# A decoder layer on one core: TensorE two expert pairs behind VectorE instead of one, with eight diagonals instead of four

## The chip, the cores and the metric

The kernel runs on one core of one Trainium2 chip. The metric is the device time of one execution in microseconds (us); less is better.

## What is computed

One decoder layer on 1024 tokens of width 1024, in float32:

```python
proj = x @ w_in                                  # split in q,k,v of attention and q,k,v,b,a,z of DeltaNet
o_attn = sliding_window_sink_attention(q_a, k_a, v_a, attn_sinks)      # window 128, 8 heads
o_dn   = gated_delta_rule(q_d, k_d, v_d, g, beta)                      # 4 heads of 128, chunks of 64
x1 = layer_norm(ALPHA * x + concat(o_attn, o_dn) @ w_out)
# PEER, per block of 128 tokens
q = (x1 @ w_query); s = q . sub_keys             # 16 lists of 128 scores for each token
vals, idx = top_k(s, 16); best, pos = top_k(vals[a] + vals[b], 16)     # 8 heads x 16 = 128 experts a token
u, v = expert_u[expert], expert_v[expert]        # rows of 1024 each
h = gelu(sum_d x1[d] * u[d]) * softmax(best)
x2 = layer_norm(ALPHA * x1 + sum_k h[k] * v[k])
```

Every token thus gathers 128 rows u and 128 rows v, 8 KB for each pair of rows.

## The kernel before

The tokens are worked in 8 blocks of 128 (NB). Each block has two kinds of work, and the kernel interleaves them on every engine:

- **The mixer**: input projection, attention, DeltaNet, output projection, first LayerNorm, expert queries, key scores and top-k. Its weights come in chunks of 1 MB: four stay in SBUF (KEPT), and the others are streamed by SyncE through two buffers `chunk`, each loaded when the product that used the buffer before is done (`chunk_used`).
- **The experts**: 128 gathers of 1 MB a block (128 rows of 8 KB each). GpSimd issues them (L445) into a **ring of 8 places** (RING, `ring`). Gather j uses place j % 8, and GpSimd waits until the gather that had the place before was added (`added`, L440; `ring_free`). The numbers of the experts come from the top-k, in four parts of 32 gathers (`staged`).

The experts go in **pairs** of gathers, 64 a block. For a pair VectorE makes two dot products of u with the tokens (L1421), ScalarE the GELU and the weighting (L994, L997) and two diagonal matrices of 128 x 64 (L1001, `diag`, DIAGS places), and TensorE multiplies the rows v by the diagonals into the PSUM sums `expert_sum` (L757, 8 matmul records). Its last matmuls raise `added`, and only they free the two places of the ring.

The order is written out by hand. `mix()` exists once for each engine and walks through the mixer with calls of `mark(name)`. The tables EARLIER and OWN say how many pairs belong to each mark: a block's first 15 pairs are done in OWN, from `top1` to `pick3`, while its own top-k still runs, and the other 49 in EARLIER, from `rope` to `pick0`, beside the mixer of the next block. At each mark VectorE and ScalarE do the pairs up to number b. **TensorE stands one pair behind**: its marks call `experts(n, b - 1)`, so that at a mark it works the pairs up to b - 1 and stops short of the one that VectorE does there.

So the ring's four pair places are, by the program, in these states when an engine stands at a mark: done by VectorE and not yet added; loaded; on the way.

Four places in the order are spoken of below.

- **The block's boundary**: the marks `sel3`, `rest3`, `pick3` (no mixer product of TensorE between them), then the `Fori` branch, then TensorE waits for `roped` (VectorE's L1187, L1188), transposes (L548, L551), and comes to the marks `rope`, `gates`, `taps1`, then the scores (L560). There are seven boundaries; five are branches back of the loop, and the first and the last lie between code that stands one behind the other.
- **The first LayerNorm**: marks `out3`, `scale1`, `shift1` without a product between, then the wait for `x1_ready` (VectorE's L1127), the transposes L504, mark `x1_T`, and the query chunks (L493).
- **The turn-over** after mark `pick0`: TensorE adds the last pairs of the older block (`experts(n - 1, PAIRS)`), VectorE reads the sums (L1439) and stages the tokens, and the pairs start from 0 again.
- **The tail**: the last block's experts from pair 15 on, with no mixer beside them.

```python
RING = 8
DIAGS = 4
OWN = {name: 1 for name in ("top1",) + NEXT_IN + AFTER_IN}
    act.wait_ge(*weighted.at(n, j + 1))
    act.wait_ge(*added.at(n, j - DIAGS + 1))
    pool.wait_ge(*added.at(n, ring_free(j)))
```

Of the kernel before, what the change touches and what calls it, by code (L numbers as in the profile page):

```python
# [28 lines left out]
P = 128  # L29
SEQ, D = 1024, 1024  # L30
NB = SEQ // P
# [4 lines left out]
DH, DK = 4, 128  # L36
CHUNK = 64
TAPS = 4
PH, KEYS, TOPK = 8, 128, 16
# [14 lines left out]
PART = SLOTS // 4  # L54
DIAGS = 4
KEPT = (0, 1, IN_CHUNKS, IN_CHUNKS + 1)
# [7 lines left out]
for _name, _width in (("ident", P), ("one", 1), ("upto", P), ("strict", P), ("same16", P), ("off32", P),  # L64
                      ("off64", P), ("same64", P), ("band", 2 * P), ("iota", TOPK),
                      ("freq", HALF), ("eps_ln", 1), ("eps_rms", 1), ("eps_l2", 1), ("ln_qscale", 1),
                      ("halves", P // 2)):
    CONSTS[_name] = (_at, _at + _width)
    _at += _width
# [3 lines left out]
def constants():  # L73

    i, j = np.arange(P)[:, None], np.arange(P)[None, :]
    same = lambda w: (i // w) == (j // w)
# [7 lines left out]
        "same16": same(16), "off32": same(32) & ~same(16), "off64": same(64) & ~same(32),  # L84
        "same64": same(CHUNK),
        "band": np.where((c > i) & (c <= i + P), 0.0, NEG),
# [56 lines left out]
def build(nc, io):  # L143
    ctx = ExitStack()
    with ctx:
# [9 lines left out]
        bank = [ctx.enter_context(nc.psum_tensor(f"bank{i}", [P, 512], F32)) for i in range(6)]  # L155
# [53 lines left out]
        def col(i, k=1):  # L209
            return small[:, i:i + k]  # L210
# [250 lines left out]
        def _(pe):  # L461
# [81 lines left out]
            def mix(n, mark, turn_over, early=False, onward=True):  # L543
# [53 lines left out]
                pe.matmul(bank[1][:, 0:DH], C["upto"], col(S_G, DH), start=True, stop=True)  # L597
                pe.matmul(bank[1][:, DH:2 * DH], C["same64"], col(S_G, DH), start=True, stop=True).then_inc(g_sums.sem, 1)
                pe.matmul(bank[0][:, :], ones, tile(A_UG), start=True, stop=True).then_inc(g_sums.sem, 1)
# [178 lines left out]
            for c in range(IN_CHUNKS):  # L778
                in_chunk(0, c, early=True)
            mix(0, Marks(own=lambda a, b: experts(0, b - 1)), lambda n: None, early=True)  # L780
            after_own = taken[0]
            with pe.Fori(1, NB - 1) as n:
                mix(n, Marks(lambda a, b: experts(n - 1, b - 1), lambda a, b: experts(n, b - 1)), turn_over)
                assert taken[0] == after_own
            mix(NB - 1, Marks(lambda a, b: experts(NB - 2, b - 1), lambda a, b: experts(NB - 1, b - 1)), turn_over, onward=False)
            pe.wait_ge(*out_ready.at(NB - 1, 0))
# [739 lines left out]
```

## Time and profile before

| | before |
|---|---|
| median of 3 runs | 3373.32 us |
| range of the 3 runs | 3371.08 to 3377.5 us |
| the profiled execution, its own time | 3375.34 us |
| its span in the trace | 3373.5 us |
| TensorE busy | 2459.0 us (73%) |
| VectorE busy | 2230.8 us (66%) |
| ScalarE busy | 1155.5 us (34%) |
| GpSimd busy | 1177.7 us (35%) |
| moved by DMA | 1254.83 MB, mean 372 GB/s |
| mean granted clock of TensorE | 0.857 |

The span is what the trace covers. The execution's own time is 1.8 us longer. A busy share is a mean over stages with different limits, so it doesn't name the bound.

### The profile page before, as it was taken

To read this page: it belongs to the slowest core of one execution; us is meant where nothing else is said; L and a number is where in the kernel's file an instruction comes from. 1 tells how busy PE (TensorE), PEld (TensorE's weight loads), DVE (VectorE), ACT (ScalarE), POOL (GpSimd) and SP (SyncE) were. 2 spreads that over 40 slices of the span, in tenths; PEclk is the share of its full clock that TensorE was granted. 3 is DMA by queue.
4 is the path that set the end of the run, shared out by engine and by line. 5 is a ranking of instruction groups with operands and counts; after the bars stand their busy time and mean duration, and the time that the engine had idled before them with its cause. 6 is when DMAs were issued, how large, how long until landed. Compare 5 with 4: busy or idle time off the path is not lost.

```text
span 3373.5 us, 40986 instructions
## 1 busy us (share of the span) xinstructions
PE 2459.0 (73%) x11840; PEld 1374.0 (41%) x11840; DVE 2230.8 (66%) x5593; ACT 1155.5 (34%) x3499; POOL 1177.7 (35%) x1028
## 2 busy tenths in 40 slices
PE   8786778857788577885788677786778867775554
PEld 6663335523355233552345333453335523351111
DVE  3267755877558765687657775587755876569444
ACT  3213532325323443225332252333532344322222
POOL 0022443224422344233542244322442234423543
PEclk8698988978889798898989888897898979887777
DMA  7049999989999899998999989998999999989997
GB/s 321 7 176 416 394 405 395 382 336 416 404 392 393 350 398 408 401 392 348 416 397 379 398 343 418 381 385 345 415 404 400 385 389 411 411 360 350 410 420 327
DMA packets 174948, 1254.83 MB, mean 372 GB/s; under 512 B 20184, under 2 KB 20312, under 8 KB 23520
## 3 DMA queue, kind: packets, MB, share of 16 engines
q0 software_dynamic: 147456, 1073.81, 78.4%
q1 hardware_dynamic: 25056, 172.66, 12.4%
q10 hardware_dynamic: 2176, 5.36, 0.4%
q8 instruction: 106, 1.74, 0.2%
q14 instruction: 154, 1.26, 0.1%
HBM read 1247.56 MB, written 4.19 MB: 371 GB/s over the span
## 4 chain that ended last, share of the span: by engine, by line
PE 31%; DMA 31%; DVE 17%; issue 10%; ACT 8%; POOL 1%; DVEq 0%; POOLq 0%; ACTq 0%; SPq 0%
DMA ring<-in_uv,expert_used 20%; PE expert_sum L757 12%; DMA chunk<-in_weights 10%; PE bank L493 7%; DVE ring L1421 7%; PE bank L485 5%; ACT diag L1001 2%; PE bank L499 2%; POOL ring L445 1%; ACT h_raw L997 1%; PE bank L504 1%; ACT L994 1%; PE bank L586 1%; PE bank L674 1%; PE bank L673 1%
## 5 line engine op out<-in xcount | busy, mean ns | idle before, releaser
L445 POOL DMA_INDIRECT ring<-in_uv,expert_used x1024 | 1177.5, 1150 | 2165.7 <-PE expert_sum L757 1661.3
L757 PE MATMUL expert_sum<-ring,diag 128*64 128x512 f32 x4096 | 1202.6, 718 | 651.3 <-ACT diag L1001 651.1
L1421 DVE CUSTOM_DVE_ANT_0 ring<-ring,x_pair 128x1024 f32<-128x1024 f32 x1024 | 1231.3, 1222 | 586.9 <-DMA ring<-in_uv,expert_used 579.7
L757 PEld LDWEIGHTS expert_sum<-ring,diag 128*64 128x64 f32 x4096 | 296.6, 156 | 1305.7 <-issue 742.0
L994 ACT ACTIVATE h_raw<-h_raw 128x2 f32<-128x2 f32 x512 | 104.4, 204 | 1542.8 <-DVE h_raw L1421 1542.3
L1001 ACT ACTIVATE diag<-const,h_raw 128x64 f32<-128x64 f32 x1024 | 298.5, 338 | 1.2 <-ACT h_raw L997 1.2
L493 PE MATMUL bank<-oT,chunk 128*128 128x128 f32 x1824 | 226.1, 285 | 37.8 <-DMA chunk<-in_weights 37.0
L997 ACT ACTIVATE h_raw<-h_raw,gate_used 128x1 f32<-128x1 f32 x1024 | 245.6, 286 | 16.7
L493 PEld LDWEIGHTS bank<-oT,chunk 128*128 128x128 f32 x1824 | 216.2, 198 | 70.6 <-DMA chunk<-in_weights 49.8
L493 PE MATMUL bank<-o_cat,chunk 128*128 128x128 f32 x1376 | 169.6, 283 | 36.4 <-DMA chunk<-in_weights 36.2
L493 PEld LDWEIGHTS bank<-o_cat,chunk 128*128 128x128 f32 x1376 | 161.7, 196 | 72.7 <-DMA chunk<-in_weights 62.8
L1144 DVE MAX8 arena<-arena 128x8 f32<-128x128 f32 (+1 forms) x384 | 103.7, 325 | 46.4 <-ACT arena L953 41.2
L499 PEld LDWEIGHTS bank<-arena 128*128 128x128 f32 x768 | 102.5, 213 | 59.0 <-issue 51.4
L499 PE MATMUL bank<-arena 128*128 128x128 f32 x768 | 114.6, 305 | 5.5 <-DVE arena L1286 1.6
L949 ACT COPY arena<-bank 128x512 f32<-128x512 f32 x32 | 18.7, 585 | 269.8 <-PE bank L493 269.8
L485 PE MATMUL bank<-chunk,o_cat 128*128 128x256 f32 x352 | 87.4, 405 | 16.2 <-DMA chunk<-in_weights 16.2
L994 ACT ACT_TABLE_LOAD x72 | 92.4, 1283 | 2.8 <-DVE h_raw L1421 1.6
L548 PE MATMUL bank<-const,arena 128*64 128x128 f32 x64 | 14.2, 399 | 107.9 <-DVE arena L1188 107.9
L485 PEld LDWEIGHTS bank<-chunk,o_cat 128*128 128x128 f32 x352 | 69.2, 202 | 38.6 <-DMA chunk<-in_weights 25.0
L1421 DVE DVE_READ_ACCUMULATOR2_ANT h_raw<- 128x1 f32 x1024 | 83.1, 81 | 0.0
L485 PE MATMUL bank<-kept,o_cat 128*128 128x256 f32 x256 | 74.5, 455 | 7.4 <-DMA kept<-in_weights 7.4
L1168 DVE SCALAR_TENSOR_TENSOR conv<-conv_in,conv_w,conv 128x128 f32<-128x128 f32 x288 | 77.8, 343 | 0.0
(237 smaller groups left out, 2539.7 us busy)
## 6 DMA issues: line engine op xcount, KB each, us to landing
chunk<-in_weights SPq DMA_DIRECT2D x137, 1024.0 KB, 10.0
ring<-in_uv,expert_used POOLq DMA_INDIRECT x1024, 11.7
ring<-in_weights SPq DMA_DIRECT2D x15, 1024.0 KB, 21.0
o_cat<-in_xT SPq DMA_DIRECT2D x8, 512.0 KB, 10.7
kept<-in_weights SPq DMA_DIRECT2D x4, 1024.0 KB, 19.1
x<-in_x SPq DMA_DIRECT2D x8, 512.0 KB, 13.6
out<-oT ACTq DMA_DIRECT2D x8, 512.0 KB, 10.2
sub_keys<-in_sub_keys ACTq DMA_DIRECT2D x1, 1024.0 KB
```

The source lines that it names most:

```text
L445: pool.indirect_dma_start(out=ring[:, (j % RING) * 2 * D:(j % RING + 1) * 2 * D], out_offset=None, in_=io["uv"], in_offset=bass.IndirectOf ...
L485: mm = pe.matmul(out, act[:, k, :], w[:, k, :], start=(k == 0), stop=(k == KT - 1))
L493: mm = pe.matmul(out, w[:, k, i * P:(i + 1) * P], act[:, k, :], start=(k == 0), stop=(k == KT - 1))
L499: mm = pe.matmul(out[:, hs], lhsT[:, hs], rhs[:, hs], start=True, stop=True)
L504: mm = pe.transpose(out[:, h * P:(h + 1) * P], in_[:, h * P:(h + 1) * P], ident)
L757: mm = pe.matmul(expert_sum[i][c * SPAN:(c + 1) * SPAN, :], diag[:, (j % DIAGS) * SPAN:(j % DIAGS + 1) * SPAN], ring3[:, j % RING, D + i * ...
L994: act.activation(h_raw[:, pair[0]:pair[1] + 1], h_raw[:, pair[0]:pair[1] + 1], ACT.Gelu).then_inc(gelued.sem, 1)
L997: act.activation(h_raw[:, j:j + 1], h_raw[:, j:j + 1], ACT.Copy, scale=gate_used[:, j:j + 1]).then_inc(weighted.sem, 1)
L1001: act.activation(diag[:, (j % DIAGS) * SPAN:(j % DIAGS + 1) * SPAN], C["halves"], ACT.Copy, scale=h_raw[:, j:j + 1]).then_inc(diag_ready.s ...
L1144: ins = dve.max(values[:, one[part]], one[2])
L1168: stt(out=convo[:, t, :], in0=conv3[:, t, k:k + P], scalar=conv_w[:, t * TAPS + k:t * TAPS + k + 1], in1=convo[:, t, :], op0=ALU.mult, op1 ...
L1421: dve.tensor_tensor_reduce(u, u, x_pair[:, (j % 2) * D:(j % 2 + 1) * D], 1.0, 0.0, ALU.mult, ALU.add, h_raw[:, j:j + 1]).then_inc(dotted.s ...
```

## The change

TensorE's marks take two pairs off instead of one, not below zero. At a mark it works the pairs up to b - 2, so that two pairs that VectorE has done stay unadded there. ScalarE's diagonals get eight places, 2 KB a partition instead of 1 KB; with them its wait at L1000 is for pair q - 4 instead of q - 2. `turn_over` and the last `experts` still work all pairs that are left.

To make room the constant `same64` goes. The sum of the gates over a chunk of 64, which was a product with it, becomes two products into the same place in PSUM, with `upto` (i <= j) and with `strict` (i > j), which together are `same64`.

```diff
-DIAGS = 4
+DIAGS = 8
...
-                      ("off64", P), ("same64", P), ("band", 2 * P), ("iota", TOPK),
+                      ("off64", P), ("band", 2 * P), ("iota", TOPK),
...
-        "same64": same(CHUNK),
...
-                pe.matmul(bank[1][:, DH:2 * DH], C["same64"], col(S_G, DH), start=True, stop=True).then_inc(g_sums.sem, 1)
+                pe.matmul(bank[1][:, DH:2 * DH], C["upto"], col(S_G, DH), start=True, stop=False)
+                pe.matmul(bank[1][:, DH:2 * DH], C["strict"], col(S_G, DH), start=False, stop=True).then_inc(g_sums.sem, 1)
...
-            mix(0, Marks(own=lambda a, b: experts(0, b - 1)), lambda n: None, early=True)
+            mix(0, Marks(own=lambda a, b: experts(0, max(b - 2, 0))), lambda n: None, early=True)
...
-                mix(n, Marks(lambda a, b: experts(n - 1, b - 1), lambda a, b: experts(n, b - 1)), turn_over)
+                mix(n, Marks(lambda a, b: experts(n - 1, max(b - 2, 0)), lambda a, b: experts(n, max(b - 2, 0))), turn_over)
...
-            mix(NB - 1, Marks(lambda a, b: experts(NB - 2, b - 1), lambda a, b: experts(NB - 1, b - 1)), turn_over, onward=False)
+            mix(NB - 1, Marks(lambda a, b: experts(NB - 2, max(b - 2, 0)), lambda a, b: experts(NB - 1, max(b - 2, 0))), turn_over, onward=False)
```

TensorE's program just behind the block's boundary, in the loop's body. L757 is a pair; L751 REGISTER_ALU stands ahead of pair 16, whose wait for its gather has a new value. Before:

```order
L757 MATMUL expert_sum<-ring,diag 64x512 x4
L752 REGISTER_ALU
L757 MATMUL expert_sum<-ring,diag 64x512 x4
L751 REGISTER_ALU
L752 REGISTER_ALU
L757 MATMUL expert_sum<-ring,diag 64x512 x4
L556 ISA
L557 REGISTER_ALU
L560 MATMUL bank<-k_keys,arena 128x256 x8
```

The same place in the change (its lines from 460 to 597 stand one lower):

```order
L757 MATMUL expert_sum<-ring,diag 64x512 x4
L752 REGISTER_ALU
L757 MATMUL expert_sum<-ring,diag 64x512 x4
L752 REGISTER_ALU
L757 MATMUL expert_sum<-ring,diag 64x512 x4
L555 ISA
L556 REGISTER_ALU
L559 MATMUL bank<-k_keys,arena 128x256 x8
L751 REGISTER_ALU
L752 REGISTER_ALU
L757 MATMUL expert_sum<-ring,diag 64x512 x4
```

Three pairs stand ahead of the scores in both. Before they are 14, 15 and 16; in the change they are 13, 14 and 15, and 16 has moved behind the scores.

TensorE's program at the turn-over: L718 are the last key scores, L514 rows for the second LayerNorm, L485 the next block's first two weight chunks. Before:

```order
L757 MATMUL expert_sum<-ring,diag 64x512 x4
L718 MATMUL bank<-sub_keys,arena 128x128 x4
L752 REGISTER_ALU
L757 MATMUL expert_sum<-ring,diag 64x512 x4
L767 REGISTER_ALU
L514 MATMUL bank<-k_keys,const 128x512 x4
L520 ISA
L485 MATMUL bank<-kept,o_cat 128x256 x8
L751 ISA
L752 ISA
L757 MATMUL expert_sum<-ring,diag 64x512 x4
L485 MATMUL bank<-kept,o_cat 128x256 x8
```

In the change:

```order
L757 MATMUL expert_sum<-ring,diag 64x512 x4
L718 MATMUL bank<-sub_keys,arena 128x128 x4
L752 REGISTER_ALU
L757 MATMUL expert_sum<-ring,diag 64x512 x4
L752 REGISTER_ALU
L757 MATMUL expert_sum<-ring,diag 64x512 x4
L767 REGISTER_ALU
L513 MATMUL bank<-k_keys,const 128x512 x4
L519 ISA
L484 MATMUL bank<-kept,o_cat 128x256 x16
L751 ISA
L752 ISA
```

Two pairs are left for the turn-over instead of one, and the next block's first pair stands behind two weight chunks instead of one.

## Rows read from the trace of the kernel before

**Rows 1.** The page: busy times of the engines.
```profile
PE 2459.0 (73%) x11840; PEld 1374.0 (41%) x11840; DVE 2230.8 (66%) x5593; ACT 1155.5 (34%) x3499; POOL 1177.7 (35%) x1028
```

**Rows 2.** The page's costliest groups: count | busy, mean ns | idle before, what ended it.
```profile
L757 PE MATMUL expert_sum<-ring,diag 128*64 128x512 f32 x4096 | 1202.6, 718 | 651.3 <-ACT diag L1001 651.1
L1421 DVE CUSTOM_DVE_ANT_0 ring<-ring,x_pair 128x1024 f32<-128x1024 f32 x1024 | 1231.3, 1222 | 586.9 <-DMA ring<-in_uv,expert_used 579.7
```

**Rows 3.** Stretches: us, busy of each engine, TensorE's granted clock, DMA share, GB/s.
```profile
1560.00:1700.00 140.00, 105.07 (x498) 49.63 (x499) 93.20 (x177) 65.66 (x198) 66.92 (x55) 0.92 1.01 418
3130.00:3330.00 200.00, 114.31 (x320) 29.27 (x320) 98.44 (x160) 46.42 (x200) 96.23 (x81) 0.76 1.01 420
1360.00:1410.00 50.00, 44.55 (x318) 33.33 (x318) 31.71 (x98) 13.38 (x44) 13.02 (x15) 1.00 0.98 396
```

**Rows 4.** The last chain in order of time, 1640 to 1680 us: start, us, what.
```profile
1647.72 1.22 DVE ring L1421
...
1650.26 3.56 PE expert_sum L757 x8
...
1655.82 11.82 DMA ring<-in_uv,expert_used
```

**Rows 5.** The same columns as rows 3, at four of the seven boundaries.
```profile
330.00:350.00 20.00, 13.87 (x58) 6.68 (x58) 19.69 (x48) 8.55 (x24) 8.96 (x8) 0.84 0.82 315
730.00:750.00 20.00, 12.61 (x51) 6.51 (x51) 15.51 (x41) 8.23 (x24) 5.29 (x4) 0.69 0.25 81
...
1530.00:1550.00 20.00, 8.29 (x34) 3.32 (x34) 11.76 (x36) 7.97 (x19) 2.58 (x3) 0.63 0.37 136
...
2740.00:2760.00 20.00, 14.72 (x58) 6.98 (x58) 19.59 (x46) 6.73 (x24) 9.74 (x8) 0.84 0.75 292
```

**Rows 6.** TensorE in order of time about 1541 us: start, us, instruction [idle before].
```profile
1519.88 3.68 PE L757 MATMUL expert_sum<-ring,diag 128*64 128x512 f32 x8 [5.54 <-ACT diag L1001]
1541.30 1.88 PE L548 MATMUL bank<-const,arena 128*64 128x128 f32 x8 [17.74 <-DVE arena L1188]
...
1543.54 4.19 PE L757 MATMUL expert_sum<-ring,diag 128*64 128x512 f32 x16
```

**Rows 7.** GpSimd, the gathers of the same stretch.
```profile
1524.37 1.97 POOL L445 DMA_INDIRECT ring<-in_uv,expert_used  x1 [5.00 <-PE expert_sum L757]
...
1546.82 0.94 POOL L445 DMA_INDIRECT ring<-in_uv,expert_used  x1 [19.24 <-PE expert_sum L757]
1548.06 0.94 POOL L445 DMA_INDIRECT ring<-in_uv,expert_used  x1 [0.30 <-PE expert_sum L757]
```

**Rows 8.** Line 445 alone, gathers issued from 1546 to 1549 us: time to landing.
```profile
DMA to landing us min/median/max: 5.7/6.5/7.4
```

**Rows 9.** VectorE in order of time, the second dot product of pair 17.
```profile
1551.09 1.21 DVE L1421 CUSTOM_DVE_ANT_0 ring<-ring,x_pair 128x1024 f32<-128x1024 f32 x1
```

**Rows 10.** All engines in order of time, at the first LayerNorm.
```profile
1353.20 1.28 DVE L1127 TENSOR_TENSOR x<-x,bank 128x512 f32<-128x512 f32 x2
...
1354.60 3.68 PE L757 MATMUL expert_sum<-ring,diag 128*64 128x512 f32 x8 [6.05 <-ACT diag L1001]
...
1358.21 1.97 PE L504 MATMUL bank<-const,x 128*128 128x128 f32 x8
```

**Rows 11.** Stretches as in rows 3, at three of the seven turn-overs.
```profile
1810.00:1840.00 30.00, 25.07 (x105) 14.06 (x103) 20.78 (x65) 10.86 (x24) 6.75 (x7) 0.89 0.84 339
2220.00:2250.00 30.00, 26.68 (x100) 15.00 (x97) 24.05 (x77) 10.27 (x23) 10.69 (x11) 0.83 0.99 407
...
3010.00:3040.00 30.00, 17.33 (x71) 7.69 (x71) 20.84 (x65) 10.16 (x23) 7.62 (x8) 0.71 0.72 282
```

**Rows 12.** All engines in order of time, a turn-over.
```profile
1417.59 2.78 DVE L1439 SCALAR_TENSOR_TENSOR oT<-x_pair,expert_sum 64x512 f32<-64x512 f32 x4 [6.96 <-PE expert_sum L757]
...
1431.11 3.68 PE L757 MATMUL expert_sum<-ring,diag 128*64 128x512 f32 x8 [4.63 <-ACT diag L1001]
...
1434.72 4.05 PE L485 MATMUL bank<-kept,o_cat 128*128 128x256 f32 x16
```

## The prediction

> **What bounds the kernel now.** I began with the page's busy times [rows 1]. No engine is above 73%, so none of them is the bound by itself. The two waits between TensorE and the experts are large [rows 2]: TensorE stood idle 651.3 us before pairs, for diagonals of ScalarE, and VectorE 579.7 us for gathers. The first invites the change: TensorE is held at a pair that isn't ready, while mixer work stands behind it in its program. Whether these waits cost time is for the DMA share to say.
>
> So I asked for stretches [rows 3]. With gathers alone, beside the mixer or without it, the DMA share is 1.01 and 418 to 420 GB/s are moved: that is what full looks like here. In the query chunks it is still 0.98. I read the chain of waits in such a stretch [rows 4] as a ring: dot product, diagonals, TensorE's pair, gather, 11.82 us until it lands, dot product again. One turn takes 20 us and serves four pairs, so 5 us a pair. A pair is 2.10 MB (two gathers of 1.05 MB), and at 419 GB/s that is 5.0 us. The 11.82 us are thus queueing behind the other gathers, and the bound is **bytes**. The 651.3 us of TensorE's waits mostly lie in stretches where DMA has no time to give.
>
> Time is then lost only where DMA runs dry. Taking 1.01 as full, the boundaries show it [rows 5]: the share is 0.25 and 0.37 over 20 us at two that are branches of the loop, and 0.82 and 0.75 at the first and the last, where no branch stands. Holes: (1.01 - 0.37) x 20 = 13 us, (1.01 - 0.25) x 20 = 15 us, 4 us and 5 us. The other three branches look like these two. A smaller hole is at the turn-over [rows 11], 5 us at the largest of the first six and 0.6 us at the smallest.
>
> Why the boundary is dry: TensorE adds pair 13 at 1519.88 us and then has nothing to do until `roped`; it adds pair 14, whose dots were long done, at 1543.54 [rows 6]. GpSimd issues no gather between the second of pair 17 (2.3 us after the row at 1524.37) and the first of pair 18 at 1546.82 [rows 7]. In these 20 us the four places hold pair 14 (done, not added), 15, 16 and 17, and when 17 has landed DMA has nothing left.
>
> **The change, part by part.**
>
> *One more place held at the boundary.* At `pick3` TensorE now stops after pair 12. Pairs 13 and 14 are both unadded while it waits for `roped`, and the gather of pair 17, which before went out at 1524.37, needs the place of 13. It goes out where before 18 did, at 1546.82. DMA's last work before the hole is one pair shorter and the hole ends at the same point of the program, so it grows by one pair: 5.0 us. I check it by landings. Gathers issued into the empty queue took 5.7 and 7.4 us [rows 8]; the second, issued at 1548.06, lands at 1555.5. Pair 17's second dot product started at 1551.09 [rows 9], so VectorE comes 4.4 us later. Both ways agree to 0.6 us, and the hole exists at all seven boundaries: 7 x 5.0 = **+35 us**, bounds 7 x 4.4 = 31 and 7 x 7.4 = 52, if a whole landing were to show. The rows are nearest to 5.0, since DMA is full again right behind the hole (rows 3's first stretch follows it).
>
> The Trainium skill, "DMA: Bandwidth & Descriptors", section Anatomy of one DMA, fits a transfer as 2.0 us and its bytes at 436 GB/s. By that the two gathers would land 2.0 + 2 x 2.4 us behind the first issue, at 1553.6, VectorE would lose 2.6 us, and the seven would cost 18 us in place of 35, an estimate. The landings of 5.7 and 7.4 us are longer than the page has it, so I keep the rows. The same page's Specifications give 358 GB/s as the HBM limit of a core; by that a pair would be 5.9 us and the seven 41 us, but the rows move 418.
>
> *A place held longer everywhere else.* In the full stretches it costs nothing, and what hides it is the queue. Pair j is added one mark later, yet TensorE no longer waits there for ScalarE. The mixer product ahead of the mark needs VectorE's step ahead of pair j + 1's dots, so it comes right behind j's own diagonals. If the shift were a whole pair (5 us), the gather would still be issued with more than one pair on the way: 11.82 us of queue less 5. The cover ends where TensorE holds pairs over 10 us, as at the boundary. The query chunks come near: TensorE is busy 44.55 of 50 us there [rows 3]. Bounds: 0, and one pair per block, 7 x 5.0 = 35 us. I take 0, since the share is 0.98 there.
>
> *TensorE's head start.* At the first LayerNorm x1 is ready after L1127 (1353.20 + 1.28 = 1354.5 us), but pair 54 is first, 3.68 us, and the transposes start at 1358.21 [rows 10]. With the change the pairs ahead of the transposes are older and done, so the transposes start near 1354.6: 3.6 us sooner, and the query chunks behind them too. At the turn-over VectorE waited 6.96 us for the last sum, which hangs on these chunks [rows 12]. It can have up to 3.6 us of that back, and the dry time there shrinks, no further than its size. The first six holes, from (1.01 - share) x 30, were 0.6 to 5.1 us, on average 2.7 us when capped at 3.6; the seventh, with a share of 0.72 [rows 11], exceeds the cap. That is 6 x 2.7 + 3.6 = 20 us at most, and 0 at least. The head start must outlive seven weight chunks, each of which waits for DMA, so I take two thirds: **-14 us**. Later at the turn-over pair 0 stands behind two weight chunks; the 4.63 us for which TensorE waited there [rows 12] now hold the second (4.05 us, the last row there), so pair 0 isn't added later.
>
> *ScalarE and the diagonals.* The wait at L1000 gets four more places and two instructions of the sequencer go. It was no wait before: TensorE's pair begins where the diagonals end. The whole stretch from the dot product's start to TensorE's is 2.54 us [rows 4], of which at most 0.1 us goes, and only in a dry stretch does it count. Bounds 0 and -0.1 x 14 = -1.4 us; I take 0. What is late next is the gather itself.
>
> *The constant.* One more product of 128 x 4 in a block of 400 us, under 0.3 us each: at most 2 us, hidden by DMA, 0. The constants' load is 64 KB shorter at the start, 0.2 us by 419 GB/s, beside the weights: 0.
>
> *The tail* has no marks; TensorE there only waits for diagonals, as before: 0.
>
> Sum, against the profiled execution of 3375.3 us: + 35 - 14 = +21, 3396 us. The median of the three runs is 2 us lower, so I predict **3394 us** for the median. About 0.2% (7 us) is what a measurement of this kernel can tell from no change.
>
> **The rivals.**
>
> *A. The shorter ring also runs dry in the chunk stretches.* From the queries to `rest3` TensorE holds pairs behind products and chunk loads. If one pair's worth of queue goes in each of seven blocks, and the head start is used up by it, the sum is 35 + 35 = +70, 3443 us; half of it with the head start kept is about +38. For it: the share is 0.98, so the queue is already near its end, and two pairs held leave two. Against: with fewer gathers queued the weight chunks land sooner, and TensorE is back sooner.
>
> *B. No change.* The hole grows by less than I say, because the first gather into an empty queue lands fast. With 2.6 us instead of 5.0 at each boundary: 18 - 14 = +4, 3377 us. Against: rows 8 and 9.
>
> *C. Faster.* The mechanism is TensorE's hold at unready pairs, in the stretch from the first LayerNorm to the third chunk of the next block. If the head start is 3.6 us at the LayerNorm and 4.6 us more at the wait for pair 0 [rows 12], and all of it comes out at the end of a block, it is 7 x 8.2 = 57 us against 35: -22, 3351 us. It decides from 5.0 us of recovered time a block. For it: VectorE and TensorE both wait at the turn-over. Against: time can only come back where DMA was dry, and the dry time outside the boundaries is some 3 us a block.
>
> *D. The change doesn't do what it says*: the place of a diagonal or the branch decides the order and TensorE's pairs come where they were. The program's order speaks against it; I give it nothing.
>
> **How the numbers follow.** My forecast (3380 to 3410) has 0.50, A 0.23, B 0.12, C 0.15. The range reaches over B and into C's smaller half, and up to the middle of A: 3362 to 3430. Leaving out half of A and the better half of C leaves out some 0.18. Faster by over 0.2% is C, 0.15; within 0.2% is B, 0.12; slower is the forecast and A, 0.73.
>
> **What would show it.** Right: the 20 us stretch at each boundary is drier by 5 us (a share of 0.12 instead of 0.37); GpSimd issues pair 17 only behind `roped`, and VectorE waits some 4 us for it at `taps1`; L504 starts right behind L1127; TensorE's wait for ScalarE at L757 falls well below 651.3 us without a gain; full stretches still show 1.01. Wrong: the share at the boundaries is unchanged (B); the query chunks show shares of 0.9 and less, or VectorE's waits for gathers grow there by 5 us a block (A); the distance between two boundaries, 400 us now, shrinks (C).

## The result, and the profile after

| | before | after |
|---|---|---|
| median | 3372.94 us (3371.08 to 3377.5, 4 runs) | 3408.47 us (3404.27 to 3414.98, 4 runs) |
| ratio, 95% interval | | 1.0105 (1.0085 to 1.0125) |
| profiled execution, own time and span | 3375.34, 3373.5 us | 3406.38, 3404.5 us |
| TensorE's mean granted clock | 0.857 | 0.844 |
| moved by DMA | 1254.83 MB, 372 GB/s | 1254.81 MB, 369 GB/s |

The change costs 35 us. It moves the same bytes and its busy times are nearly the same. The page after, busy times and costliest groups, against [rows 1, 2]:

```profile
PE 2462.1 (72%) x11856; PEld 1395.9 (41%) x11856; DVE 2239.3 (66%) x5593; ACT 1143.3 (34%) x3499; POOL 1150.0 (34%) x1028
...
L1421 DVE CUSTOM_DVE_ANT_0 ring<-ring,x_pair 128x1024 f32<-128x1024 f32 x1024 | 1237.8, 1224 | 823.7 <-DMA ring<-in_uv,expert_used 817.1
L757 PE MATMUL expert_sum<-ring,diag 128*64 128x512 f32 x4096 | 1175.4, 708 | 416.4 <-ACT diag L1001 416.2
```

TensorE's wait for diagonals fell from 651.1 to 416.2 us, and VectorE's wait for gathers rose from 579.7 to 817.1. One fell by 235 us, the other rose by 237, and the kernel is slower. This is the first reading: **a wait that shrinks is no gain if it only moves to the engine that feeds the ring.**

The stretches after, columns as in [rows 3, 5]. The first three answer to rows 3, the other four to the boundaries of rows 5, each taken at the same distance from its `roped` (the boundaries come at other times now):

```profile
1580.00:1720.00 140.00, 110.61 (x496) 54.00 (x496) 88.93 (x160) 65.20 (x192) 57.79 (x52) 0.85 0.99 404
3160.00:3360.00 200.00, 111.92 (x322) 28.46 (x320) 98.26 (x161) 46.42 (x200) 98.22 (x80) 0.77 1.01 420
1363.00:1413.00 50.00, 43.16 (x299) 33.04 (x298) 25.86 (x83) 11.36 (x40) 12.38 (x12) 0.97 0.95 375
...
319.60:339.60 20.00, 15.08 (x58) 7.05 (x58) 14.53 (x39) 7.81 (x22) 8.33 (x7) 0.77 0.52 200
722.10:742.10 20.00, 12.66 (x50) 6.50 (x50) 12.11 (x36) 7.89 (x19) 4.86 (x5) 0.68 0.22 71
1535.20:1555.20 20.00, 8.73 (x35) 3.71 (x36) 12.42 (x39) 8.34 (x21) 2.16 (x3) 0.61 0.22 77
2755.90:2775.90 20.00, 15.81 (x63) 7.47 (x65) 13.83 (x36) 6.19 (x20) 8.01 (x8) 0.84 0.55 205
```

Full is full still (0.99 and 1.01). The boundary is drier: 0.82 to 0.52 and 0.75 to 0.55 where no branch stands (6 and 4 us), 0.25 to 0.22 and 0.37 to 0.22 at branches. The query chunks fell from 0.98 to 0.95.

TensorE in order of time about the boundary at 1546.3 us, against [rows 6]:

```profile
1523.52 2.77 PE L757 MATMUL expert_sum<-ring,diag 128*64 128x512 f32 x6
1546.47 1.89 PE L547 MATMUL bank<-const,arena 128*64 128x128 f32 x8 [20.18 <-DVE arena L1188]
1548.15 0.64 PE L550 MATMUL bank<-const,arena 128*64 128x128 f32 x2
1548.71 6.34 PE L757 MATMUL expert_sum<-ring,diag 128*64 128x512 f32 x24
```

GpSimd's gathers there, against [rows 7], and the landings of the two issued from 1552 to 1554 us, against [rows 8]:

```profile
1528.37 1.16 POOL L444 DMA_INDIRECT ring<-in_uv,expert_used  x1 [0.30 <-issue]
1552.43 0.94 POOL L444 DMA_INDIRECT ring<-in_uv,expert_used  x1 [22.90 <-PE expert_sum L757]
1553.67 0.97 POOL L444 DMA_INDIRECT ring<-in_uv,expert_used  x1 [0.30 <-PE expert_sum L757]
```

```profile
DMA to landing us min/median/max: 5.6/6.3/7.1
```

VectorE there: L1175 and L1176 are its first two instructions behind the branch, the two dot products are pair 17's, which did not wait at all in [rows 9].

```profile
1541.01 0.16 DVE L1175 TENSOR_TENSOR small<-arena,dt_b 128x4 f32<-128x4 f32 x1 [5.09 <-issue]
1543.37 0.17 DVE L1176 TENSOR_SCALAR small<-small 128x4 f32<-128x4 f32 x1 [2.19 <-issue]
...
1558.06 1.23 DVE L1421 CUSTOM_DVE_ANT_0 ring<-ring,x_pair 128x1024 f32<-128x1024 f32 x1 [2.92 <-DMA ring<-in_uv,expert_used]
...
1560.78 1.22 DVE L1421 CUSTOM_DVE_ANT_0 ring<-ring,x_pair 128x1024 f32<-128x1024 f32 x1 [1.48 <-DMA ring<-in_uv,expert_used]
```

So pairs 13, 14 and 15 are added only behind `roped` (the 24 matmul records at 1548.71), pair 17's gather goes out at 1552.43, and VectorE waits 2.92 + 1.48 = 4.4 us for it: the mechanism that was forecast. This place is the cheapest of the seven. Over all of them VectorE waits 4.4 to 6.0 us for pair 17's two gathers, 37.6 us in all, and in the kernel before it doesn't wait for them at any. The same place in the kernel before shows what nobody forecast, L1176's wait:

```profile
1533.27 0.16 DVE L1175 TENSOR_TENSOR small<-arena,dt_b 128x4 f32<-128x4 f32 x1 [5.10 <-issue]
1538.20 0.17 DVE L1176 TENSOR_SCALAR small<-small 128x4 f32<-128x4 f32 x1 [4.76 <-issue]
```

The first LayerNorm in order of time, against [rows 10]; then TensorE and VectorE at the turn-over, against [rows 12]:

```profile
1356.89 1.28 DVE L1127 TENSOR_TENSOR x<-x,bank 128x512 f32<-128x512 f32 x2
...
1358.23 1.97 PE L503 MATMUL bank<-const,x 128*128 128x128 f32 x8 [5.99 <-DVE x L1127]
```

```profile
1419.59 3.65 PE L757 MATMUL expert_sum<-ring,diag 128*64 128x512 f32 x16
...
1423.31 2.78 DVE L1439 SCALAR_TENSOR_TENSOR oT<-x_pair,expert_sum 64x512 f32<-64x512 f32 x4 [2.86 <-PE expert_sum L757]
```

The transposes stand right behind L1127 (0.06 us instead of 3.7), as forecast. But from x1 to the sums it takes 1423.3 - 1358.2 = 65.1 us now, 1417.6 - 1354.5 = 63.1 us before. The head start did not arrive.

**Three legs of a block.** For the experiments I cut each block at three instructions of VectorE: `roped` (end of L1188), x1 ready (end of L1127), sums (start of L1439). These are means over the six or seven blocks of each profile, in us; the period is the distance of two `roped`. "Lag" is how many pairs TensorE stands behind. Each line is one execution. The time ahead of the first boundary is in none of the legs, and it moves from run to run: the first transposes of x1 start at 182.3 us in the kernel before, 171.4 in the change, 175.7 in e1, 173.4 in e4 (which keeps the old constants) and 180.2 in e11. So the 11 us by which they came sooner in the change, which e1's expectation asks about, come and go between runs.

| kernel | roped to x1 | x1 to sums | sums to roped | period |
|---|---|---|---|---|
| before | 215.0 | 64.2 | 121.8 | 401.3 |
| the change | 218.8 | 65.1 | 122.5 | 405.7 |
| e1, all but the lag | 214.4 | 64.4 | 122.5 | 401.2 |
| e2, lag 2 at pick3 only | 221.1 | 64.0 | 120.1 | 405.5 |
| e9, lag 3 at pick3 only | 230.0 | 64.5 | 117.8 | 411.9 |
| e4, lag 0 at pick3 only | 214.9 | 64.3 | 122.0 | 401.2 |
| e8, e4 with TensorE kept at work | 214.9 | 63.9 | 122.4 | 400.0 |
| e3, lag 2 but at pick3 | 213.9 | 65.7 | 123.9 | 403.5 |
| e5, lag 2 at scale1, shift1 only | 214.9 | 64.0 | 122.4 | 400.8 |
| e6, lag 2 from rope to out3 only | 214.8 | 64.3 | 122.0 | 401.8 |
| e7, lag 2 from x1_T to rest3 only | 214.2 | 65.8 | 124.1 | 404.0 |
| e10, lag 0 from x1_T to rest3 only | 212.5 | 71.8 | 124.7 | 408.1 |

### The profile page after: what moved, and what is told of

Its sections match the earlier page's. It is cut to its first block, busy times and chain, and to the rows that moved or that the text cites. A ratio compares the mean times of both kernels' runs of the same rounds, so it can differ in the third digit from the quotient of the medians.

```text
span 3404.5 us, 41738 instructions
## 1 busy us (share of the span) xinstructions
PE 2462.1 (72%) x11856; PEld 1395.9 (41%) x11856; DVE 2239.3 (66%) x5593; ACT 1143.3 (34%) x3499; POOL 1150.0 (34%) x1028
## 2 busy tenths in 40 slices
DMA packets 174954, 1254.81 MB, mean 369 GB/s; under 512 B 20184, under 2 KB 20312, under 8 KB 23520
## 4 chain that ended last, share of the span: by engine, by line
DMA 34%; PE 31%; DVE 17%; issue 10%; ACT 5%; POOL 2%; DVEq 0%; ACTq 0%; POOLq 0%; SPq 0%
DMA ring<-in_uv,expert_used 25%; PE expert_sum L757 11%; PE bank L492 10%; DMA chunk<-in_weights 9%; DVE ring L1421 6%; PE bank L484 3%; PE bank L498 2%; POOL ring L444 2%; ACT diag L1001 1%; DVE arena L1144 1%; PE bank L503 1%; ACT arena L861 1%; PE bank L674 1%; PE bank L673 1%; PE bank L585 1%
## 5 line engine op out<-in xcount | busy, mean ns | idle before, releaser
L444 POOL DMA_INDIRECT ring<-in_uv,expert_used x1024 | 1149.8, 1123 | 2222.6 <-PE expert_sum L757 1763.3
L1421 DVE CUSTOM_DVE_ANT_0 ring<-ring,x_pair 128x1024 f32<-128x1024 f32 x1024 | 1237.8, 1224 | 823.7 <-DMA ring<-in_uv,expert_used 817.1
L757 PE MATMUL expert_sum<-ring,diag 128*64 128x512 f32 x4096 | 1175.4, 708 | 416.4 <-ACT diag L1001 416.2
L757 PEld LDWEIGHTS expert_sum<-ring,diag 128*64 128x64 f32 x4096 | 299.6, 156 | 1067.0 <-issue 752.5
L492 PE MATMUL bank<-o_cat,chunk 128*128 128x128 f32 x1376 | 186.0, 300 | 69.5 <-DVE oT L1127 34.8
L492 PEld LDWEIGHTS bank<-o_cat,chunk 128*128 128x128 f32 x1376 | 178.0, 213 | 105.2 <-issue 55.4
L1421 DVE DVE_READ_ACCUMULATOR2_ANT h_raw<- 128x1 f32 x1024 | 84.0, 82 | 0.0
L513 PE MATMUL bank<-k_keys,const 8*128 8x512 f32 x128 | 75.7, 741 | 10.9 <-ACT arena L921 10.9
## 6 DMA issues: line engine op xcount, KB each, us to landing
ring<-in_weights SPq DMA_DIRECT2D x15, 1024.0 KB, 21.6
```

Of the source, the lines that this page charges most:

```text
L444: pool.indirect_dma_start(out=ring[:, (j % RING) * 2 * D:(j % RING + 1) * 2 * D], out_offset=None, in_=io["uv"], in_offset=bass.IndirectOf ...
L492: mm = pe.matmul(out, w[:, k, i * P:(i + 1) * P], act[:, k, :], start=(k == 0), stop=(k == KT - 1))
L513: mm = pe.matmul(banks[i][:, :], ident[LN_ROWS, k:k + 1].to_broadcast([8, P]), k_keys[LN_ROWS, :], start=True, stop=True)
L757: mm = pe.matmul(expert_sum[i][c * SPAN:(c + 1) * SPAN, :], diag[:, (j % DIAGS) * SPAN:(j % DIAGS + 1) * SPAN], ring3[:, j % RING, D + i * ...
L1421: dve.tensor_tensor_reduce(u, u, x_pair[:, (j % 2) * D:(j % 2 + 1) * D], 1.0, 0.0, ALU.mult, ALU.add, h_raw[:, j:j + 1]).then_inc(dotted.s ...
```

## The experiments

A cost in us is taken from the ratio, and can differ from the difference of the medians by some us. Beside e1 to e4 the kernel before had a median of 3368.53 us, beside e5 to e8 3371.07, beside e9 and e10 3368.96, beside e11 and e12 3368.65. Except for e4, e8 and e12, each edit starts from the changed kernel and sets how many pairs TensorE takes off, by the number b of pairs at a mark: rest3 is 14, pick3 15, rope 16, out3 54, scale1 55, shift1 56, x1_T 57, pick0 64, and top1 is 1 again. In the kernels so edited some lines stand three higher than in the change (L1424 is L1421 there, L1178 is L1175).

### e1: everything but the lag

```diff
-max(b - 2, 0)
+max(b - 1, 0)
```

> Eight diagonals, no same64, but TensorE one pair behind as before. Theory 1 (places of the ring that are held cost DMA time, nothing else of the change does): 3373 us, within 5 us of before, and 0.37 or so of DMA share in the 20 us at a branch. Theory 2 (the added product, the diagonals or the shorter constants move the time): over 5 us from before. The first block's transposes of x1 came 11 us sooner with the change (171 instead of 182 us): if that is the constants' or the product's doing, it shows here as 3363 us; if it is chance of the clock, it comes and goes between runs.

3368.9 us, ratio 0.9999 (0.9985 to 1.0014). The diagonals, the constant and the two products cost nothing together. All 35 us are TensorE's lag. This kernel is the base for the other legs.

### e2 and e3: the boundary alone, and all but the boundary

```diff
-max(b - 2, 0)
+max(b - (2 if b == 15 else 1), 0)    # e2
+max(b - (1 if b == 15 else 2), 0)    # e3
```

> As e1, but at the mark pick3 alone TensorE stays two pairs behind, so that pairs 13 and 14 are held over the block's boundary. Theory 1: the boundary alone costs 7 x 5.0 us of dry time, less some 2.6 us at each of the five branches where VectorE's second idle time at the branch (L1176) falls from 4.8 to 2.15 us: 3373 + 22 = 3395 us. Rival (the boundary is neutral, since the shorter fetch and the head start give it back, and the cost of the change sits in the query and input chunks): 3375 to 3380 us.

> The change, but at pick3 TensorE catches up to one pair behind, so that only pair 14 is held over the boundary. Theory 1: the 22 us of the boundary come back, 3408 - 22 = 3386 us, the dry time at the boundaries is 75 us again and L1176's idle time 4.8 us. Rival (chunks, not the boundary): 3403 to 3408 us.

e2: 3399.84 us, 1.0087 (1.0059 to 1.0114), so the boundary alone costs 29 us. e3: 3395.84 us, 1.0085 (1.0057 to 1.0114), so the rest costs as much again by its ratio, 29 us, though its profiled run is the fastest of its four (3382.57 us; the others took 3391.92 to 3400.71) and shows half of it. The boundary alone and all but the boundary are 29 + 29 = 58 us, and the change, which has both, costs 35. The gap of 23 us is wider than the intervals make likely, and nothing here shows where it comes from. Either way the prediction's forecast that the rest is a gain fell, and the next runs cut it up.

In the table e2's leg behind `roped` is 6.7 us longer than e1's and its leg ahead of it 2.4 us shorter. The shorter one is the branch: VectorE's waits there (in all, times, longest), in e1 and in e2:

```profile
DVE small L1178 <- issue: 25.1, 5, 5.2
DVE small L1179 <- issue: 24.0, 5, 5.0
```

```profile
DVE small L1178 <- issue: 24.7, 5, 5.1
DVE small L1179 <- issue: 10.9, 5, 2.3
```

6.7 x 7 = 47, less 24.0 - 10.9 = 13 us, is 34 against the 29 measured and the 29.3 between the spans (3400.6 and 3371.3). The forecast had only the first kind. In the change the leg is 4.4 us longer than e1's, not 6.7; in e2 three of the seven stretches behind `roped` (12 to 60 us) ran at a clock of 0.65 to 0.75 and were some 4 us drier.

### e4: none held at the boundary (from the kernel before)

```diff
+def upto(b):
+    return max(b - (0 if b == 15 else 1), 0)
...
-mix(n, Marks(lambda a, b: experts(n - 1, b - 1), lambda a, b: experts(n, b - 1)), turn_over)
+mix(n, Marks(lambda a, b: experts(n - 1, upto(b)), lambda a, b: experts(n, upto(b))), turn_over)
```

> The kernel before, but at pick3 TensorE also adds pair 14, for which it waits some 5 us that it would spend idle before roped anyway. Theory 1: the gather of pair 18 goes out before the boundary, each hole is one pair shorter (5.0 us, or the 4 us that the first hole has), 3373 - 34 = 3339 us, and L1176's idle time stays at 4.8 us since DMA is busy longer. Rival (the hole isn't set by held places but by VectorE's branch, so that DMA makes up nothing): 3370 to 3376 us.

A miss: 3379.56 us, 1.0032 (1.0013 to 1.0051). Over 34 us at each of the seven boundaries, the dry time (1.01 less the share, by the length) fell from 80.9 us in e1 to 58.8. But most of it came back right behind: in the 48 us that follow (12 to 60 us behind `roped`) the dry time rose from 2.4 us in e1 to 18.2, the leg from `roped` to x1 is no shorter, and the period is e1's. (The 11 us by which the median is slower aren't in the profiled run, whose span is 3369.1 us; where they go is open.) In its profile two of the seven boundaries stood out by the clock. Stretches 28 us long at the same distance from `roped`, at the third and the fourth boundary, then TensorE and VectorE at the fourth:

```profile
1162.00:1190.00 28.00, 21.36 (x98) 9.46 (x98) 17.49 (x38) 25.23 (x60) 11.93 (x11) 0.94 0.99 394
1562.00:1590.00 28.00, 23.48 (x81) 11.43 (x81) 16.50 (x37) 21.58 (x56) 10.86 (x9) 0.64 0.83 322
```

```profile
1574.83 7.09 PE L586 MATMUL bank<-v_rows,arena 128*128 128x64 f32 x32
1581.85 3.68 PE L757 MATMUL expert_sum<-ring,diag 128*64 128x512 f32 x8
```

```profile
1581.96 0.69 DVE L1233 TENSOR_TENSOR o_cat<-bank,small 128x512 f32<-128x512 f32 x1 [9.15 <-PE bank L586]
```

Here the products of attention (32 records) ran at the lower level (1.2 GHz, a granted clock of 0.5) and took 7.09 us; at the fourth boundary of the kernel before they took 3.79, and VectorE waited 4.83 us for them instead of 9.15. That gave a theory: the gain was there and the clock took it. The traces spoke against it already, since the kernel before has two such boundaries too: its products take 7.09 us at the third and the fifth, in e4 at the first and the fourth.

### e8: e4 with TensorE kept at work at the boundary

From e4, behind the mark pick3:

```diff
+if onward:
+    for _ in range(8):
+        pe.matmul(bank[0][:, :], ident, const[:, 0:512], start=True, stop=True)
```

> The kernel before with pair 14 added ahead of the boundary (as in the run that brought nothing), and eight matmuls of 128 x 512 behind it whose result nobody reads, to keep TensorE at work while it waits for roped. Theory 1 (the expected gain was lost to the clock: the products behind the boundary, 32 of L586, took 7.1 us instead of 3.8 where the granted clock had fallen): the granted clock from 12 to 60 us behind roped is 0.86 or more at all seven boundaries, dry time there falls from 18 to 5 us, and the kernel is 10 to 25 us faster than before, 3345 to 3360. Theory 2 (the clock is chance, and the mixer's chain gives the gain back anyway): same as without the matmuls, 3370 to 3380.

The eight products did their part at six of the seven boundaries. TensorE (L1194 is L1188 here), and the stretch behind the fourth boundary:

```profile
1519.22 8.08 PE L746 MATMUL bank<-const 128*128 128x512 f32 x16
1528.83 1.03 PE L548 MATMUL bank<-const,arena 128*64 128x128 f32 x8 [1.53 <-DVE arena L1194]
```

```profile
1541.00:1589.00 48.00, 31.97 (x134) 12.99 (x134) 35.83 (x79) 31.95 (x85) 20.53 (x18) 0.89 0.98 389
```

The transposes take 1.03 us instead of 1.88, and the clock is 0.89 (in the same 48 us of e4 it is 0.72). Over the seven boundaries the clock there is 0.89 or more at six, and 0.79 at the last. The dry time from 12 to 60 us behind `roped` is 1.0 to 1.4 us at the five branches, but 4.3 and 7.7 at the first and the last boundary, and 18.2 in all, as in e4. Yet the kernel takes 3380.71 us, 1.0023 (1.0004 to 1.0042), no faster than e4. The clock theory falls: at the fourth boundary the clock rose and the dry time went from 5.3 to 1.4 us, and the mean leg behind `roped` is 214.9 us in both. What e4 and e8 share is VectorE's pace. From pair 15's dot products to pair 22's it takes 34.4 us in the kernel before, 33.8 in e4, 35.3 in e8; to pair 29's 72.3, 72.6 and 73.4. In none of them does VectorE wait for a gather at pairs 15 to 18: between their dot products it does the mixer's gates, convolution and scores, and the next gathers wait for the places of these pairs. More loaded pairs don't help an engine that isn't waiting for them. This reading fits the four kernels; no run made VectorE itself faster there. In the change, where it does wait, the two distances are 39.3 and 77.9.

### e9: three held at the boundary

```diff
-max(b - 2, 0)
+max(b - (b - 12 if b in (14, 15) else 1), 0)
```

> Three pairs behind at pick3 (12, 13 and 14 wait for roped), one everywhere else. The gathers of pair 16 too go out only behind roped. Theory 1 (behind the boundary VectorE has no slack for a gather that comes late, so each place held costs a pair, and once DMA is empty at the branch VectorE's second wait there is short): VectorE waits for pair 16 at gates, the hole grows by another 5 us at each boundary, both of VectorE's waits at the branch are 2.2 us (first and second, 5.0 and 4.7 in the kernel before) where DMA is already empty at the first, so 5 x 3 us come back: 29 + 35 - 15 = about 50 us slower than before, 3415 to 3430. Theory 2 (one hold was the whole effect, and the further one hides in the same hole): as with two pairs at pick3, about 30 us slower, 3400. If VectorE's waits at the branch don't go with the empty queue, the first stays at 5.0 and the sum is 29 + 35 = 64.

3445.65 us, 1.0215 (1.0171 to 1.0259): 72 us slower. The first theory's mechanism holds, its size was short (50 expected). VectorE behind the branch, and at pair 16:

```profile
1558.78 0.16 DVE L1178 TENSOR_TENSOR small<-arena,dt_b 128x4 f32<-128x4 f32 x1 [2.27 <-issue]
1561.03 0.17 DVE L1179 TENSOR_SCALAR small<-small 128x4 f32<-128x4 f32 x1 [2.08 <-issue]
...
1575.58 1.23 DVE L1424 CUSTOM_DVE_ANT_0 ring<-ring,x_pair 128x1024 f32<-128x1024 f32 x1 [8.29 <-DMA ring<-in_uv,expert_used]
...
1578.85 1.23 DVE L1424 CUSTOM_DVE_ANT_0 ring<-ring,x_pair 128x1024 f32<-128x1024 f32 x1 [2.04 <-DMA ring<-in_uv,expert_used]
```

Both waits at the branch are 2.1 to 2.3 us now, as the first theory said. The leg behind `roped` is 15.6 us longer than e1's, 109 us in seven blocks; the waits at the branch, 11.3 and 10.6 us in all against 25.1 and 24.0, give 27 back. That is 82 against 78 us between the spans (3449.4 and 3371.3). The price per place isn't constant: from none held to one nothing is lost (e4), the second costs 29 us, the third 43 more. VectorE's wait for the gathers that come late has the same steps: none in the kernel before, 38.2 us in all for pair 17 in e2, 76.8 for pair 16 in e9.

### e5, e6, e7: the rest of the change, cut in three

```diff
-max(b - 2, 0)
+max(b - (2 if b in (55, 56) else 1), 0)         # e5, and e11 once more
+max(b - (2 if 16 <= b <= 54 else 1), 0)         # e6
+max(b - (2 if b >= 57 or b < 15 else 1), 0)     # e7
```

> Two pairs behind at the marks scale1 and shift1 alone, one everywhere else; eight diagonals. The transposes of x1 stand ahead of pair 54 and nothing else moves. Theory 1 (the prediction's step, head start): the query chunks and the last sum of a block come up to 3.6 us sooner and the dry time at the turn-over shrinks, about 14 us faster than before, 3355 (down to 3350). Theory 2 (the pair is only passed on: TensorE is busy 44.55 of 50 us in the query chunks, so pair 54's time comes back ahead of the last sum, and the transposes and the first query product run at a granted clock of 0.5): the stretch from the transposes to the sums is 4 us longer, the distance from x1 to the sums the same within 1 us, time unchanged, 3365 to 3375.

> Two pairs behind at the marks rope to out3 alone (pairs 16 to 53), one everywhere else. Theory 1 (the prediction's step: in the full stretches the queue of 11.8 us hides it): no difference, within 5 us of before. Theory 2 (a place held longer costs at each small disturbance): 5 to 15 us slower, with dry time of more than 20 us in all between the boundaries and x1_T.

> Two pairs behind from the mark x1_T to the mark rest3 (but not at pick3), one from pick3 to shift1. Theory 1 (rival A of the prediction: the ring runs dry in the chunk stretches when a place is held longer): most of what the run with one pair at pick3 alone still lost is found here, 15 to 25 us slower than before (3385 to 3395), with more dry time in the input chunks. Theory 2 (the chunk stretches lose nothing): within 5 us of before.

e5: 3365.28 us, 0.9981 (0.9962 to 1.0). e6: 3368.66 us, 1.0001 (0.9984 to 1.0018). e7: 3386.59 us, 1.0049 (1.0031 to 1.0067).

e6 confirms the queue as cover in the full stretches. It also shows the first reading by itself: TensorE's wait for diagonals falls from 646.9 us in e1 to 480.1, VectorE's wait for gathers rises from 566.4 to 725.3, and the time stays. e7 costs 16 us. That is about what e3's profiled run lost (14 us), and not the 29 of its ratio: e5, e6 and e7 together have every lag of e3 and add up to 10 us, so some 18 us of e3's cost are in none of its parts, and where they come from is open. e7 goes with its first theory, the mechanism of rival A at half its price: 1.4 us more from x1 to the sums and 1.6 more behind them. The 70 us and more of input chunks, from 30 us behind the sums to 22 ahead of `roped`, in e1 and in e7:

```profile
1442.24:1513.92 71.68, 53.19 (x306) 33.21 (x304) 57.65 (x190) 17.90 (x68) 20.70 (x20) 0.91 1.01 416
```

```profile
1437.27:1511.45 74.18, 55.34 (x308) 36.27 (x306) 58.02 (x190) 18.12 (x69) 24.62 (x21) 0.90 0.96 388
```

With one pair behind, DMA is full there (1.01), with two it is not (0.96). A pair waits for TensorE behind a chunk product: in e7 pairs 2 to 9 of the fourth block are added 4.3 to 9.0 us after their diagonals are ready, in e1 0.1 to 5.0 us.

e5 moves the transposes forward by 3.6 us (0.1 us behind x1 instead of 3.7), and x1 to sums takes 64.0 us instead of 64.4. Nine tenths are given back, most likely because the pair that stood ahead of the transposes now stands between them and the last sum, on an engine that is busy 44.55 of 50 us there [rows 3]. The 30 us behind the sums and the stretch from the transposes to the sums, in e1 and in e5:

```profile
1412.24:1442.24 30.00, 26.47 (x96) 15.67 (x96) 28.29 (x87) 8.68 (x22) 6.37 (x6) 0.83 0.89 348
1351.54:1412.24 60.70, 53.96 (x371) 39.22 (x370) 33.91 (x104) 17.29 (x53) 19.46 (x18) 0.98 0.97 388
```

```profile
1403.65:1433.65 30.00, 26.86 (x92) 16.12 (x94) 28.29 (x87) 8.79 (x22) 7.98 (x8) 0.77 1.01 411
1341.18:1403.65 62.47, 56.38 (x377) 39.89 (x378) 37.59 (x111) 18.53 (x58) 16.30 (x17) 0.97 0.91 367
```

The hole behind the sums closes (0.89 to 1.01) and the query chunks ahead of them get drier (0.97 to 0.91). Over seven blocks the dry time behind the sums falls from 28.8 to 8.4 us, and from x1 to the sums it rises from 21.9 to 43.5: it moved, and hardly any was won.

### e11: e5 once more

> The kernel with two pairs behind at scale1 and shift1 alone, once more, to tell 0 from -6 and from -14 us. Theory 1 (the head start is worth what the prediction took): 14 us faster, a ratio of 0.996. Theory 2 (most of it is given back, because pair 54 now stands between x1 and the last sum, in a stretch where TensorE is busy): 0 to 6 us faster, 0.998 to 1.000.

3365.49 us, 0.9984 (0.996 to 1.0008). With e5 it says about 6 us faster, at the edge of what can be told from no change; -14 (0.9958) lies outside both intervals. It is the one version that beats the kernel before and the change, if anything does.

### e10: none held in the chunk stretches

```diff
-max(b - 2, 0)
+max(b - (0 if b >= 57 or b < 15 else 1), 0)
```

> TensorE level with VectorE (no pair behind) from x1_T to rest3, one behind from pick3 to shift1. Theory 1 (in the chunk stretches a place held longer costs what the run with two there lost, 16 us, and it goes the other way too): the ring gets its place back sooner, and the kernel is up to 15 us faster than before, 3355 to 3365. Theory 2 (with none behind TensorE stands at a pair whose diagonals aren't ready, and the weight chunks and key scores behind it come later): 10 to 40 us slower than before, with TensorE's wait for ScalarE's diagonals above 651 us and the stretch from the transposes to the sums over 424.7 us long.

3429.93 us, 1.0165 (1.012 to 1.0209), 56 us slower, more than either theory had, in the second's direction. The group of L757 on its page, and the 30 us behind the sums:

```profile
L757 PE MATMUL expert_sum<-ring,diag 128*64 128x512 f32 x4096 | 1212.3, 724 | 786.1 <-ACT diag L1004 774.7
```

```profile
1423.52:1453.52 30.00, 21.13 (x70) 11.28 (x72) 28.29 (x87) 8.90 (x22) 6.36 (x6) 0.74 0.68 259
```

TensorE's wait for diagonals went from 651.1 to 774.7 us, and from the transposes to the sums it takes 476.4 us over the seven blocks instead of 424.7, as the second theory said. And this time it cost: x1 to sums takes 7.4 us more than e1's, and the dry time in the 30 us behind the sums is 79.8 us in all instead of 28.8. So here the wait that the change removes is a real one, and one pair behind already removes it.

### e12: a ring of six (from the kernel before)

```diff
-RING = 8
+RING = 6
```

> The kernel before with a ring of six places, three pairs, TensorE one behind as before (the weights of the first block get fewer places at the start too, so the first 300 us aren't compared). Theory 1 (two pairs behind is the same as one pair place less, everywhere): at the boundary and in the chunk stretches as the change, and in the full stretches nothing: about 30 us at the boundaries, 16 in the chunk stretches, 3405 to 3425. Theory 2 (a place that is really gone costs in the full stretches too: 11.8 us of queue less 5 is 6.8, and a gather into the empty queue takes 5.7 to 7.4): the DMA share in the full stretches falls under 1.0 and the kernel is over 80 us slower, above 3450.

3655.22 us, 1.0841 (1.0802 to 1.088), 283 us slower: the second theory. Two full stretches, the second in the tail:

```profile
1700.00:1840.00 140.00, 95.09 (x440) 45.41 (x437) 81.67 (x143) 51.03 (x159) 56.78 (x51) 0.89 0.94 364
3400.00:3600.00 200.00, 109.67 (x276) 26.33 (x272) 86.25 (x139) 39.46 (x170) 74.25 (x69) 0.65 0.96 365
```

With one pair place really gone, even gathers alone run at 0.96 and 365 GB/s instead of 1.01 and 420. Two pairs behind is not the same as one place less: in a full stretch of the change (pairs 29 to 39 of the fourth block) a pair is added 0.1 to 4.1 us after its diagonals are ready, so the place is lent for a part of a pair's 5 us, not for all of them.

## Why the prediction was right, and where it was not

Forecast 3394 us, +21 against the profiled 3375; measured +35. The parts measured alone are 29 (boundary), 16 (chunk stretches), 0 (full stretches), 0 (diagonals and constant) and -6 (head start), 39 in sum against 35 of the whole. This sum leaves out e3, which has all but the boundary in one kernel and cost 29 us where its parts add up to 10. With it the whole would be 58.

- **What bounds the kernel**: right for time lost, wrong for time won. "Time is then lost only where DMA runs dry" holds, but filling the dry time is no gain by itself (e4, e8): behind the boundary the pace is VectorE's own, by the reading of e4 and e8, and only a gather that comes later than its turn is felt. The price of a place is one-sided.
- **One more place held at the boundary**, +35, bounds 31 to 52: mechanism right, with pair 17's gather behind `roped` and VectorE's wait of 4.4 to 6.0 us for it, 37.6 in all. e2 gives 29, since the term lacked the branch, where VectorE gets 13 us back. The Trainium skill, "DMA: Bandwidth & Descriptors", Anatomy of one DMA, would have the two gathers landed 2.0 + 2 x 2.4 = 6.8 us behind the first issue, an estimate; they took 1560.78 - 1552.43 = 8.35 us, and the measurement decides.
- **The forecast share of 0.12** in place of 0.37 was 0.22, and 0.22 in place of 0.25 at another branch: the reasoning left out that L1176's wait would shrink by 2.6 us. Over 34 us, 22 ahead of `roped` to 12 behind, the hole at the fourth boundary grew from 12.9 to 16.0 us, 3.1 in place of 5.0. At the two boundaries without a branch the loss was 6 and 4 us, as forecast.
- **A place held longer everywhere else**, 0, bounds 0 and 35: right in the full stretches (e6), wrong in the chunk stretches, 16 us (e7). The step that failed is "I take 0, since the share is 0.98 there": 0.98 showed the queue at its end, not its reserve. It was also read at the query chunks alone, and much of the loss is in the input chunks, where the share was 1.01 in e1 and is 0.96 in e7.
- **TensorE's head start**, -14, bounds 0 to -20: the step that failed is the cap by the dry time at the turn-over. That hole did shrink, by the 20 us that the cap allowed (28.8 to 8.4 in e5), but the sums came only 0.4 us sooner, and 21.6 us of dry time turned up ahead of them. Dry time that shrinks at one place was taken for time won. The head start is worth about 6 us, by two runs whose intervals reach from -13 to +3.
- **ScalarE and the diagonals, the constant**: 0, right (e1).
- **The tail**: from the last turn-over to the end it is 355.4 us before, 358.0 in e1 and 360.4 in the change. That is no cost that can be told: e2, which has e1's lag there, takes 360.8 us, and e3 and e7, which have the change's from x1_T on, take 356.7 and 356.9. It was not tried alone.
- **Rivals**: A had the right place and twice the price; its half with the head start kept, +38, is nearer to the 35 than the forecast's +21. C's mechanism is real and small; B did not happen. TensorE's wait fell to 416 us "without a gain", as said.

The forecast came out 14 us low: 16 us missed in the chunk stretches, 8 too many expected of the head start, 6 too many charged at the boundary and 4 left over between parts and whole. That 3408 still lies in the forecast's own band (3380 to 3410) is luck in part: the two errors of 24 us one way were met by 10 the other way, and one of its terms (0 for the chunk stretches) belongs to rival A.

## What to carry to other kernels

Read a consumer's wait together with the wait of the engine that refills its buffers. Standing further behind only helps where the work ahead of the mark is late, and every stage may want its own distance: here one pair everywhere, two at most ahead of the first LayerNorm. Dry time of the bounding resource says where time can be lost; filling it is a gain only if the engine that consumes the data is waiting for it there, and it has to be counted over the whole block, since it can turn up at the next place. Work moved behind a milestone on a busy engine comes back ahead of the next one.

## What the runs showed of the hardware

- **The wait behind a loop's branch depends on the DMA queue.** VectorE's first two instructions there wait 5.0 and 4.7 us for "issue" where gathers are in flight (before, e1, e4), 5.0 and 2.2 us where the queue has run empty between the two (the change, e2), and 2.3 and 2.1 us where it is empty ahead of both (e9, as its expectation said). There are five branches in each; the long first waits are 4.5 to 5.2 us, the long second ones 4.7 to 5.0, the short ones 2.1 to 2.4. The likely reason is that the code's own loads stand behind the gathers' packets, and the traces bear it out. In each wait a queue of the kind `instruction` (q14) moves 8 KB packets, two in each wait of the kernel before, e1, e4 and e9. In the first three kernels the second of them starts 2.8 to 3.1 us after the wait begins, in e9 0.3 to 0.5 us after it, and from there to the end of the wait it is 1.6 to 2.2 us in all four. So the part that changes with the queue lies ahead of these packets. That they are VectorE's own code is inferred from when they come.
- **Half the clock is seen in single products.** The 32 records of attention took 3.79 us at 2.4 GHz and 7.09 at 1.2, the 8 transposes behind `roped` 1.03 and 1.88. The transposes ran at the lower level (a granted clock of 0.5) at all seven boundaries of the kernel before, where TensorE had stood idle for 8.0 to 19.7 us ahead of them, and the products of attention, some 38 us later, at two of the seven, without a difference in the idle time that would say which two. Eight products put into that idle time in e8 kept the transposes at 1.03 us and the products of attention at 3.79 at six of the seven boundaries each, and gained nothing in time.
